# A hybrid decoder layer on one core: two homes of up's input forms swapped, transfers reordered, split weights shared by two gate rounds

## The reference

```python
u = rmsnorm(h, g_mix);  z = u @ w_in                   # 2048 x 7184
y = concat(hgrn2(z), gla(z))                           # two groups of recurrent heads
h = h + y @ w_out                                      # 2048 x 2048
m = rmsnorm(h, g_mlp) @ w_up                           # 2048 x 8192, "up"
h = h + square(relu(m)) @ w_down                       # 8192 x 2048, "down"
gate = sigmoid(rmsnorm(h, g_ple) @ w_pg)               # 2048 x 2048
h = h + gate * (p @ w_pp)                              # 256 x 2048
return rmsnorm(h, g_final)
```

## Time and profile before

| | |
|---|---|
| time, median of 3 runs | 2482.71 us (2482.13 to 2483.28) |
| the profiled execution | 2482.57 us, its span 2480.6 us |
| TensorE matmuls | 2436.7 us busy, 98% of the span, 13711 instructions |
| DVE | 1932.4 us, 78% |
| ACT | 1208.7 us, 49% |
| POOL | 152.3 us, 6% |
| HBM read, written | 306.85 MB, 67.11 MB |

### The profile page before, as it was taken

One profiled execution on the slowest core, in us unless ns is written; L12 is line 12 of the kernel. 1 busy time (PEld: TensorE's weight loads), 2 busy tenths in 40 slices (PEclk: granted clock), 3 DMA queues, 4 the chain that ended last, 5 costly groups with the idle time before them and its releaser, 6 DMA issues.

```text
span 2480.6 us, 35403 instructions
## 1 busy us (share of the span) xinstructions
PE 2436.7 (98%) x13711; PEld 2122.4 (86%) x13711; DVE 1932.4 (78%) x2382; ACT 1208.7 (49%) x1791; POOL 152.3 (6%) x152
## 2 busy tenths in 40 slices
PE   8999999999999999999999999989999999999996
PEld 7888888888888887999999999978888888888885
DVE  6766666688888436888888888879999999995457
ACT  6444444444444334666666666643333433345345
POOL 5111111111110000000000000000000000000111
PEclk9999999999999999999999999999999999999999
DMA  5323223332232433666666666686654665533323
GB/s 172 85 68 85 68 71 81 85 85 69 70 82 81 157 119 119 176 194 192 192 193 197 202 199 201 218 326 229 229 185 164 237 229 212 211 133 121 113 94 119
DMA packets 382462, 375.82 MB, mean 152 GB/s; under 512 B 5564, under 2 KB 311384, under 8 KB 380280
## 3 DMA queue, kind: packets, MB, share of 16 engines
q1 hardware_dynamic: 382064, 373.90, 47.0%
q10 hardware_dynamic: 264, 0.08, 0.0%
HBM read 306.85 MB, written 67.11 MB: 151 GB/s over the span
## 4 chain that ended last, share of the span: by engine, by line
PE 61%; DVE 3%; DMA 1%; ACT 1%; issue 1%; DVEq 0%; ACTq 0%
PE bank L2217 20%; PE bank L2219 20%; PE bank L2218 20%; DMA ring<-in_w_down 1%; DVE w_lo L2099 0%; DVE w_lo L1961 0%; PE bank L2591 0%; DMA w_raw<-in_w_up 0%; DMA ring<-in_w_pg 0%; DVE h L2128 0%; DVE w_lo L1828 0%; ACT w_hi L1310 0%; PE bank L2490 0%; DVE gate_e L2121 0%; DVE gate_e L2119 0%
## 5 line engine op out<-in xcount | busy, mean ns | idle before, releaser
L2217 PE MATMUL bank<-u_hi,w_hi 128*128 128x512 f32 x896 | 364.0, 406 | 0.2
L2217 PE MATMUL bank<-w_hi,forms 128*128 128x512 f32 x896 | 350.7, 391 | 8.1 <-DVE h L2007 8.1
L2219 PE MATMUL bank<-u_hi,w_lo 128*128 128x512 f32 x896 | 350.4, 391 | 0.0
L2218 PE MATMUL bank<-u_lo,w_hi 128*128 128x512 f32 x896 | 349.5, 390 | 0.0
L2219 PE MATMUL bank<-w_hi,forms 128*128 128x512 f32 x896 | 349.5, 390 | 0.0
L2218 PE MATMUL bank<-w_lo,forms 128*128 128x512 f32 x896 | 349.4, 390 | 0.0
L2217 PE MATMUL bank<-xs,w_hi 128*128 128x256 f32 x1024 | 289.7, 283 | 2.2 <-issue 2.2
L2218 PE MATMUL bank<-xs,w_hi 128*128 128x256 f32 x1024 | 289.6, 283 | 0.0
L2219 PE MATMUL bank<-xs,w_lo 128*128 128x256 f32 x1024 | 289.5, 283 | 0.0
L1245 ACT ACTIVATE w_hi<-ring 128x1024 fp32r<-128x1024 f32 x126 | 133.9, 1065 | 221.7 <-PE bank L2219 135.0
L1433 DVE TENSOR_TENSOR w_lo<-w_raw,w_hi 128x2048 fp32r<-128x2048 f32 x70 | 163.8, 2340 | 73.4 <-ACT w_hi L861 73.4
(11 more groups left out here) (302 smaller groups left out, 5382.1 us busy)
## 6 DMA issues: line engine op xcount, KB each, us to landing
w_raw<-in_w_in SPq DMA_DIRECT2D x56, 1024.0 KB, 5.6
forms_scratch<-stage SPq DMA_DIRECT2D x32, 1792.0 KB, 11.5
forms<-forms_scratch SPq DMA_DIRECT2D x56, 1024.0 KB, 7.2
ring<-in_w_down SPq DMA_DIRECT2D x39, 1024.0 KB, 5.1
w_raw<-in_w_up SPq DMA_DIRECT2D x32, 1024.0 KB, 7.8
raw<-in_w_up SPq DMA_DIRECT2D x32, 1024.0 KB, 7.9
w_raw<-in_w_down SPq DMA_DIRECT2D x25, 1024.0 KB, 5.2
ring<-in_w_pg SPq DMA_DIRECT2D x20, 1024.0 KB, 5.0
```

Of the source, the lines that this page charges most:

```text
L2217: pe.matmul(ps, whi, xhi, start=start, stop=False, skip_group_check=shared)
L2218: pe.matmul(ps, whi, xlo, start=False, stop=False, skip_group_check=shared)
L2219: return pe.matmul(ps, wlo, xhi, start=False, stop=stop, skip_group_check=shared)
```

## The change

1. **Homes.** x11 (product 0's form) moves to the place of h's tiles 0 to 7, x22 (product 6's) into `xd` where x11 was. x11 is done with earlier in a pair than x22. r5(0) moves from `ring` to `raw2[:, 1]`, where h3 comes back.
2. **Transfers at the change to down.** h0 is loaded after slot 0 of up's last pair and h1 after slot 1, form 2 with forms 0 and 1, and h3 behind r21 of group 1. h2 stays among the forms.
3. **Start of up.** The split of x22 gets functions of its own (`x_last_hi`, `x_last_lo`) and a semaphore of its own; for the last two indices it comes behind the sums. DVE's order of `up_lo`, `up_sum` and `add_out` changes. TensorE takes index 6 for products 0 and 1 and then index 7. ACT's first copy out of PSUM waits for `x22_ready`.
4. **Gate rounds 3 and 4.** Round 3 takes its half units in the order 4 to 7, 0 to 3; round 4 takes 0 to 3 first and multiplies by the halves that round 3 left in `w_hi` and `w_lo`. So places 0 to 3 of round 4 have no split and no load (18 loads of w_pg instead of 20). Tile 2 of round 2 is added at place 5 and tile 3 at place 0 of round 4.

The core of the diff (unchanged lines are mostly left out):

```diff
@@ -268,7 +268,7 @@
         xd = at("xd", region1, [P, 2, KT // 2, 2, HALF], F32R)
-        x22 = at("x22", region1 + KT * D, [P, KT // 2, 2, HALF], F32R)
+        x11 = at("x11", region1 + KT * D, [P, KT // 2, 2, HALF], F32R)
@@ -343,6 +343,7 @@
         h_turned, x_raw, x_step, xs_sum = sem("h_turned"), sem("x_raw"), sem("x_step"), sem("xs_sum")
+        x22_hi, x22_ready = sem("x22_hi"), sem("x22_ready")
@@ -434,7 +435,7 @@
         def r5(G):
-            return ring[:, 2, :] if G % 2 else w_raw[:, 0, :] if G else ring[:, 0, :]
+            return ring[:, 2, :] if G % 2 else w_raw[:, 0, :] if G else raw2[:, 1, :]
@@ -451,10 +452,10 @@
-            if j < 2:
-                return xd[:, j, i, lo, :]
-            if j == 6:
-                return x22[:, i, lo, :]
+            if j == 0:
+                return x11[:, i, lo, :]
+            if j in (1, 6):
+                return xd[:, 1 if j == 1 else 0, i, lo, :]
@@ -528,6 +529,23 @@
+        def place_in(r, pos):
+            return pos if pos < 4 else pos - 1
+        def half_unit_of(r, pos):
+            z = place_in(r, pos)
+            return (z + 4) % 8 if r == LAST - 1 else z
+        def quad_of(r, pos):
+            return NT * r + (place_in(r, pos) // 2 if r < LAST else place_in(r, pos) // 2 - 2)
+        def split_of(r, pos):
+            return gate_hu(r, pos) - (4 if r == LAST else 0)
@@ -657,30 +675,32 @@
+            def load_h(b):
+                sp.dma_start(h[:, 4 * b:4 * b + 4, :], h_dram[b]).then_inc(h_back[b], 16)
+            sp.wait_ge(up_done, last_pair + 1)
+            load_h(0)
...
-            def load_h(b):
-                sp.dma_start(h[:, 4 * b:4 * b + 4, :], h_dram[b]).then_inc(h_back[b], 16)
+            load_h(1)
...
             load_form(0, 1)
+            load_form(0, 2)
             sp.wait_ge(up_done, UP_SLOTS)
-            load_h(0)
-            load_form(0, 2)
+            load_form(0, 3)
             store_forms(UP_PAIRS - 2)
-            load_form(0, 3)
...
             load_form(0, 5)
-            load_h(1)
             load_form(0, 6)
-            load_h(3)
...
                 n, q = NT * r + i, ROUNDS[r][0]
+                if r >= LAST - 1:
+                    i = (i + 2) % 4
@@ -718,6 +738,8 @@
                 load_down(r21(G + 1), G + 1, 1, 0, w21_landed)
+                if G == 0:
+                    load_h(3)
@@ -726,7 +748,7 @@
             sp.dma_start(g_out[:, :], g_final.partition_broadcast(P)).then_inc(g_landed, 16)
-            for n in range(3, 4 * (LAST + 1)):
+            for n in range(3, NT * LAST + 2):
@@ -1081,6 +1103,7 @@
                     act.wait_ge(xd_ready, i - 1)
+                    act.wait_ge(x22_ready, i - 1)
@@ -1091,13 +1114,16 @@
                 act.wait_ge(x_raw, 2 * i + 1)
+                if i == 0:
+                    act.wait_ge(h_saved[0], 32)
+                    act.wait_ge(mix_squared, 2 * NT)
...
                 act.activation(form_up(1, i, 0), r21x, ACT.Copy).then_inc(xd_hi, 1)
-                if i == 0:
-                    act.wait_ge(h_saved[0], 32)
-                    act.wait_ge(mix_squared, 2 * NT)
-                act.activation(form_up(6, i, 0), r22x, ACT.Copy).then_inc(xd_hi, 1)
+            def x_last_hi(i):
+                act.activation(form_up(6, i, 0), blocks_of_x(i)[3], ACT.Copy).then_inc(x22_hi, 1)
@@ -1137,12 +1163,14 @@
                         x_direct_hi(i)
+                        x_last_hi(i)
...
                         x_direct_hi(i)
+                        x_last_hi(i)
@@ -1158,6 +1186,8 @@
             x_sums_hi(6)
+            x_last_hi(6)
+            x_last_hi(7)
@@ -1204,7 +1234,7 @@
                         act.wait_ge(xs_sum, KT // 2)
-                        act.wait_ge(xd_ready, KT // 2)
+                        act.wait_ge(x22_ready, KT // 2)
@@ -1297,16 +1327,15 @@
             def gate_hi(r, pos):
-                s, q = gate_hu(r, pos), ROUNDS[r][0]
-                act.wait_ge(half_done, s - 3)
+                s, q = split_of(r, pos), ROUNDS[r][0]
+                act.wait_ge(half_done, gate_hu(r, pos) - 3)
...
                 else:
-                    z = pos if pos < 4 else pos - 1
-                    n = NT * r + z // 2
+                    n = quad_of(r, pos)
                     act.wait_ge(pg_landed[n % 3], 16 * (n // 3 + 1))
-                    src = part(ring[:, n % 3, :], z % 2)
+                    src = part(ring[:, n % 3, :], place_in(r, pos) % 2)
@@ -1371,11 +1400,15 @@
                     square_out(q, 2)
-                    square_out(q, 3)
+                    if r < LAST - 2:
+                        square_out(q, 3)
...
                 for pos in range(GATE_HUS):
-                    gate_hi(r, pos)
+                    if r < LAST or pos >= 4:
+                        gate_hi(r, pos)
+                    if r == LAST and pos == 1:
+                        square_out(2, 3)
@@ -1808,12 +1841,16 @@
                 r11x, r12x, r21x, r22x = blocks_of_x(i)
-                v.wait_ge(xd_hi, 3 * i + 1)
+                v.wait_ge(xd_hi, 2 * i + 1)
                 v.tensor_tensor(form_up(0, i, 1), r11x, form_up(0, i, 0).bitcast(F32), ALU.subtract)
-                v.wait_ge(xd_hi, 3 * i + 2)
-                v.tensor_tensor(form_up(1, i, 1), r21x, form_up(1, i, 0).bitcast(F32), ALU.subtract)
-                v.wait_ge(xd_hi, 3 * i + 3)
-                v.tensor_tensor(form_up(6, i, 1), r22x, form_up(6, i, 0).bitcast(F32), ALU.subtract).then_inc(xd_ready, 1)
+                v.wait_ge(xd_hi, 2 * i + 2)
+                v.tensor_tensor(form_up(1, i, 1), r21x, form_up(1, i, 0).bitcast(F32), ALU.subtract).then_inc(xd_ready, 1)
+            def x_last_lo(i):
+                v.wait_ge(x22_hi, i + 1)
+                v.tensor_tensor(form_up(6, i, 1), blocks_of_x(i)[3], form_up(6, i, 0).bitcast(F32), ALU.subtract)\
+                    .then_inc(x22_ready, 1)
@@ -1864,35 +1901,39 @@
                         x_direct_lo(i)
+                        x_last_lo(i)
...
                         x_direct_lo(i)
+                        x_last_lo(i)
...
                     x_sums_lo(3)
-                    up_sum_3(0)
-                    up_sum_1(0)
             up_lo(0)
-            up_sum_2(0)
+            up_lo(1)
             add_out(NT - 1, 0)
-            up_lo(1)
-            up_sum_4(0)
+            up_sum_3(0)
+            up_sum_1(0)
...
             add_out(NT - 1, 2)
+            up_sum_2(0)
...
             up_lo(3)
+            x_direct_lo(6)
             x_sums(6)
-            x_direct_lo(6)
...
             x_sums_lo(7)
+            x_last_lo(6)
+            x_last_lo(7)
+            up_sum_4(0)
@@ -1965,7 +2006,7 @@
                 else:
-                    v.wait_ge(up_done, UP_SLOTS - PRODUCTS + 1)
+                    v.wait_ge(up_lo_ready, UP_SLOTS - 1)
@@ -2089,13 +2130,12 @@
             def gate_lo(r, pos):
-                s = gate_hu(r, pos)
+                s = split_of(r, pos)
...
                 else:
-                    z = pos if pos < 4 else pos - 1
-                    src = part(ring[:, (NT * r + z // 2) % 3, :], z % 2)
+                    src = part(ring[:, quad_of(r, pos) % 3, :], place_in(r, pos) % 2)
@@ -2150,8 +2190,9 @@
                     gate_clamp(q, 3)
+                if at == (5 if r == LAST - 2 else 4):
                     gate_add(q, 2)
-                if at == 5:
+                if at == 5 and r < LAST - 2:
@@ -2159,7 +2200,10 @@
                         add_products((s - 5) // 2)
-                    gate_lo(r, pos)
+                    if r < LAST or pos >= 4:
+                        gate_lo(r, pos)
+                    if r == LAST and pos == 0:
+                        gate_add(2, 3)
@@ -2535,7 +2579,7 @@
                     if p == 0:
-                        pe.wait_ge(xd_ready if j in (0, 1, 6) else xs_ready, i + 1)
+                        pe.wait_ge(x22_ready if j == 6 else xd_ready if j < 2 else xs_ready, i + 1)
@@ -2546,8 +2590,9 @@
             up_product(0, 1, range(0, 6))
-            up_product(0, 0, range(6, 8))
-            up_product(0, 1, range(6, 8))
+            for i in (6, 7):
+                for j in (0, 1):
+                    up_product(0, j, (i,))
@@ -2607,10 +2652,10 @@
             def gate_half(r, pos, between=(), tokens=None):
-                s, (q, tiles) = gate_hu(r, pos), ROUNDS[r]
+                s, (q, tiles) = split_of(r, pos), ROUNDS[r]
...
                 pe.wait_ge(half_lo, s + 1)
-                z = pos if pos < 4 else pos - 1
+                z = half_unit_of(r, pos)
```

## The result

The changed kernel takes 2468.31 us, median of 6 runs (2467.27 to 2469.1), where the kernel before took 2482.38 (2480.54 to 2483.28) on the same chips: a ratio of 0.9944, 95% interval 0.9932 to 0.9956, 14.1 us less. The forecast was 2469.9, 12.8 us less than 2482.7. The profiled execution took 2468.48 us, its span 2466.4.

A forecast was written before the change was run, and what follows sets the result against it. TensorE, busy for 98% of the span, was taken as the bound, so only its idle and slow stretches could be won. Gains of 9.2 + 0.0 + 3.6 = 12.8 us gave 2469.9 us, range 2466.3 to 2474.5.

The forecast's parts named there:

- 1, change to down: Change to down: reordered loads land r11 of group 1 9.0 us earlier; gain 9.2 us (7.5 to 10.6).
- 2, order at the start of up: Start of up: the new order lets TensorE restart at 995.3 instead of 996.94; gain 1.6 us.
- 2, slow clock: Start of up: the clock falls in one gathered idle stretch of 3.9 us; price 1.6 us (0 to 2.2).
- 3, gate rounds: Last two gate rounds: fewer halves and loads shorten round 3's gate chain; gain 3.6 us (2.5 to 4.6).
- The margin of 0.5: Change to down: form 0 lands at 1631.7 and is needed at 1632.2, 0.5 us later.
- rival B: Change to down: a new stall, with form 0 3 us late and r11 later as well; 2475 us, chance 0.12.
- r21: free: Change to down: r21 of group 1 lands at about 1671.4, split needed by 1675.8, splits take 2.3; no cost.
- rival A: Start of up: the clock doesn't fall, 1.6 us more gain; 2468.3 us, chance 0.29.
- Rival D: Start of up: the clock falls and stays down; slower from 29 us on, forty give 2488; chance 0.02.
- The place 5 wait: Round 3, place 5: TensorE's wait stays, as ACT's high half starts behind tile 3's inverse; 0.1 us gained.
- one stretched step less: Gate rounds: upper bound, POOL stretches one DVE addition step less; gain 4.6 us.
- Rival C: Gate rounds: sharing the halves gives nothing, as round 3's gate chain holds TensorE; 2473.5 us, chance 0.07.

The follow-up runs named there:

- e1_transfers: The kernel before with only the swapped homes of x11 and x22, r5(0)'s new home and the new transfer order; 2472.49 us, ratio 0.9955.
- e5_warm: The changed kernel with 24 more matmuls that nothing reads between products 1 and 2 of up; 2467.06 us, ratio 0.9935.
- e3_rounds: The kernel before with only the shared halves of gate rounds 3 and 4; 2478.68 us, ratio 0.998.
- e6_form6_late: The changed kernel with form 6 loaded behind r11 of group 1 instead of ahead of it; 2471.29 us, ratio 0.995.
- e2: The kernel before with only the new steps at the start of up; 2483.01 us, ratio 0.9997.
- e4: The changed kernel with the load of h1 put back in front of form 6; 2471.68 us, ratio 0.9949.
- e7: The changed kernel with ACT's high half of round 3, place 5, ahead of tile 3's exponential and inverse; 2466.01 us, ratio 0.9932.
- e11: The e1_transfers kernel profiled a second time, no edit; 2475.47 us.
- e8: The changed kernel with x22's last two low halves ahead of the sums' last two on DVE; 2466.75 us, ratio 0.9935.
- e9: The changed kernel with both x22's last low halves ahead of the sums' and place 5's high half ahead of tile 3's exponential; 2464.15 us, ratio 0.9926.
- e12: The kernel before, unchanged, profiled a second time; 2482.42 us.

## Why the prediction was right, and where it was off

| term | predicted | measured | from |
|---|---|---|---|
| 1, change to down | 9.2 (7.5 to 10.6) | 9.8 alone; 9.8 of the 10.2 in D to G | e1_transfers, stages |
| 2, order at the start of up | 1.6 | 1.6 (T to P) | stages of before and after |
| 2, slow clock | -1.6 (0 to -2.2) | -1.7 | P to D, e5_warm |
| 3, gate rounds | 3.6 (2.5 to 4.6) | 3.4 in G to E and 0.4 ahead of G; 3.6 to 3.8 alone | stages, e3_rounds |
| not forecast | 0 | 0.7 | up to T, code that is the same |
| sum | 12.8 | 14.2 of span, 14.1 of medians | |

**Part 1.** The queue was worked out at 2.65 us per MiB, and with a full queue the loads landed 2.5 to 2.7 apart. Form 0 was to land at 1631.7 and landed at 1623.1 + 8.5 = 1631.6, the very moment at which half unit 0 started. The margin of 0.5 was used up: down's first matmul starts 0.27 behind up's last one (1631.34, 1631.61), where the two are 0.12 apart in the kernel before. That is 0.15 us, so rival B, a stall of up to 3 us, did not come. r11 was to land at 1661.5 and landed at 1660.3, and this is the term that was mis-sized, by 1.2. The landings say which loads were faster: form 1 came 2.6 us behind form 0 (3.4 predicted), the store took 4.8 (5.1), and the six loads from the store to r11 took 15.5 (15.9); form 3, 3.4 behind form 2 (2.7 predicted), was slower. Half unit 18 was to start 21.2 behind r11's landing and started 21.3 behind it (1681.57 - 1660.3). The stall left before it was to be about 1.3 and is 0.7. "r21: free" was right for this order, but e6_form6_late shows how thin it is. Two small slips of the prediction change nothing: DVE's last split ended at 1659.7 by the row and not at 1659.6, and r11's late bound is 1663.3 to 1663.4 by its own terms and not 1663.2.

**Part 2.** The wait of the transposes was to go, and went; TensorE was to restart 1.6 us earlier, and T to P is 91.8 instead of 93.4. One idle stretch of about 4 us was to gather (3.9 predicted, 4.05 found) and the clock was taken to fall, at 1.6 us: it fell, at 1.7 (1.2 to 2.7 over the five profiles with this stretch). Of all terms this one was the guess, and that it came out within 0.1 is luck: the other profiles of this stretch had it up to 0.5 cheaper and 1.0 dearer. e5_warm shows that the fall is that cost, since filling the stretch gives back exactly P to D of before. So rival A, no fall, did not come: the five profiles with an idle stretch of 4.05 us (after, e2, e4, e6, e7) all show a fall, and the mean clock was 0.996 or 0.997 in all six timed runs of the changed kernel, where it was 0.998 in all five with TensorE kept busy. That the measured 2468.3 is rival A's number to the tenth is chance; it is made up of a fall that did come and of gains elsewhere. Rival D needed 29 us of slow clock; there were 3.6 behind the restart. One line of this step was misread: a stretch longer than 3.9 us does stand in the trace of before besides the one of 8.13, TensorE's wait of 4.4 us for its first load at the very start, where the windows show 1.00. It touches no term of the sum.

One **reading under this step was wrong**, though it did not spoil the sum. From 2.45 and 2.17 us idle at 1.00 I read that such stretches keep the clock. They do so in some executions. These are all idle stretches of 1.8 to 2.6 us behind T, in us:

| | clock fell | clock stayed at 1.00 |
|---|---|---|
| start of up | 2.14, 2.15 (e1), 2.23, 2.16 (e11), 2.50 (e8), 2.51 (e9), 2.16 (e12) | 2.45, 2.17 (before), 2.20, 2.15 (e3), 2.02 (e12) |
| half unit 18 | 1.93 (e4) | 1.98 (e6) |
| place 6 of round 3 | 1.87 (e1), 1.86 (e11), 1.87 (e2) | 1.87 (before), 1.87 (e12) |

The length does not tell the two columns apart. The kernel with part 1 alone fell at all six of its places in two profiles, the kernel before at one of six; whether its order makes a fall likelier is not shown by so few. The Trainium skill, page "TensorE: Matmul & The Clock Gate", Part 1, says that the monitor runs free of the kernel, so that the same kernel meets it at different points. The prediction cited it as shown by no run. e12_before_again agrees with it in what comes of it (how the monitor works no run here shows): the same kernel, the same stretch to 0.01 us, once at 1.00 and once with 0.59 over the 4 us from 996 on, 1.5 us apart. It also means that the kernel before pays for such falls in part of its executions, which is in its median and was in no term of my sum. Of its stretches of 1.87 us and more behind T (2.45, 2.17, 8.13 and the 1.87 of place 6) the changed kernel has none; it has one of 4.05.

**Part 3.** The place 5 wait was to gain 0.1 and lost 0.3 (1.24 before, 1.54 after), since ACT's high half starts 2.1 behind G and not 1.7; place 6 was to come 1.0 earlier and came 0.7 earlier; the second addition of round 3 was to end 3.6 earlier and ended 3.4 earlier; the restart, read off at 2443.81 + 10.8 = 2454.6, was to be 2454.4. One step of that addition is still stretched, 1.67 beside 0.69, while POOL works from 2432.08 to 2433.73, and it ends 0.55 behind POOL, as the stretched steps of the earlier trace rows do. So the bound "one stretched step less" did not come. The Trainium skill, page "GPSIMD Engine Reference", section 1, names this contention, and the trace agrees again. Rival C, sharing gives nothing, is out by e3_rounds alone.

**The missing 1.3 us** (1.4 of span) are 0.7 from the start of the kernel, where nothing was changed, 0.6 from the change to down and 0.3 from the gate rounds, less 0.2 at the start of up. A forecast against one profiled execution cannot do better than that start varies: 901.7 to 903.6 over fourteen profiles.

## What to carry to other kernels

Where an engine stands still for a load that was issued in time, count the MiB ahead of it in the queue and move out what is not needed soon; then work out which load is late next, because there is always one. Gathering several short stalls into one longer one can cost as much as it gains, since TensorE's clock may fall in the long one (2483.01 against 2482.25 us); the better order takes the work that nobody waits for out of the chain, as x22's low halves and place 5's high half did here (4.2 us). Where such a stall can't be removed, unneeded matmuls in it cost nothing here and kept the clock up (1.7 us for the one of 4.05 us, 1.5 in P to D for the one of 2.5).
